# Seven block products in place of eight for part of an MLP's second projection, inside a fused two-layer kernel on one core

## The reference, cut to what matters

```python
def squared_relu_mlp(h, w1, w2):            # h 256x2048, w1 2048x8192, w2 8192x2048
    return jnp.square(jax.nn.relu(h @ w1)) @ w2

x = x + squared_relu_mlp(h, w_mlp_in[l], w_mlp_out[l])
return rmsnorm(x, norm_final)               # then the second layer starts
```

## Time and profile before

| | |
|---|---|
| median of 3 runs (lowest, highest) | 1685.77 us (1685.72, 1685.93) |
| the profiled execution's own time | 1685.47 us |
| its span, first to last instruction | 1683.7 us |
| TensorE matmul busy, share of span | 1674.5 us, 99% |
| weight load (PEld), DVE, ACT, POOL busy | 86%, 67%, 49%, 3% |
| granted TensorE clock | 1.00 of full |
| DMA: moved, mean rate | 361.47 MB, 215 GB/s |

### The profile page before, as it was taken

The page is one execution under the profiler, slowest core; times in us unless marked ns, Lnnn a source line. Parts: engine busy times, 40 slices in busy tenths (PEclk is TensorE's granted clock), DMA queues, the critical chain, the costliest instruction groups (busy, mean ns, idle before and its releaser), DMA issues.

```text
span 1683.7 us, 25495 instructions
## 1 busy us (share of the span) xinstructions
PE 1674.5 (99%) x9397; PEld 1454.5 (86%) x9397; DVE 1125.7 (67%) x1148; ACT 823.6 (49%) x1085; POOL 56.8 (3%) x64
## 2 busy tenths in 40 slices
PE   9999999999999999999999999999999999999998
PEld 7888888888888888888888888799999988888886
DVE  5554546557877777777877777775675556757754
ACT  5645754554445444444445445454444454444443
POOL 1000000000000000000000000000000001101100
PEclk9999999999999999999999999999999999999999
DMA  9643545567777787767777777675555655555562
GB/s 305 221 132 115 189 138 175 163 206 268 260 258 261 271 277 279 252 231 279 266 266 257 265 260 254 215 233 170 171 167 176 196 188 190 179 194 173 196 205 88
DMA packets 171691, 361.47 MB, mean 215 GB/s; under 512 B 11008, under 2 KB 17472, under 8 KB 171344
## 3 DMA queue, kind: packets, MB, share of 16 engines
q1 hardware_dynamic: 169392, 352.37, 62.7%
q0 software_dynamic: 2064, 7.56, 1.3%
q10 hardware_dynamic: 144, 0.26, 0.0%
HBM read 358.00 MB, written 2.15 MB: 214 GB/s over the span
## 4 chain that ended last, share of the span: by engine, by line
PE 98%; DVE 1%; issue 1%; ACT 0%; POOLq 0%; POOL 0%; ACTq 0%; DVEq 0%
PE G L759 31%; PE S L759 13%; PE S L773 12%; PE G L773 12%; PE G L742 10%; PE G L776 6%; PE S L776 6%; PE S L712 2%; PE G L748 1%; PE S L1144 0%; PE S L797 0%; DVE window_sums L1849 0%; PE S L1137 0%; PE S L1123 0%; PE S L1011 0%
## 5 line engine op out<-in xcount | busy, mean ns | idle before, releaser
L1462 DVE TENSOR_TENSOR w_lo<-raw,w_hi 128x1024 fp32r<-128x1024 f32 (+1 forms) x573 | 702.7, 1244 | 403.1 <-ACT w_hi L1178 402.5
L1178 ACT ACTIVATE w_hi<-raw 128x1024 fp32r<-128x1024 f32 (+1 forms) x574 | 588.5, 1045 | 519.5 <-PE G L759 131.0
L759 PE MATMUL G<-w_hi,X_pair 128*128 128x512 f32 (+2 forms) x1456 | 444.6, 384 | 0.0
L759 PEld LDWEIGHTS G<-w_hi,X_pair 128*128 128x128 f32 x1456 | 269.6, 188 | 55.2 <-issue 3.3
L759 PE MATMUL G<-w_lo,X_pair 128*128 128x512 f32 (+2 forms) x728 | 276.8, 380 | 0.0
L773 PE MATMUL S<-Y_pair,w_hi 128*128 128x512 f32 x768 | 267.0, 390 | 0.0
L773 PE MATMUL G<-Y_pair,w_hi 128*128 128x512 f32 x768 | 266.8, 390 | 0.0
L776 PE MATMUL G<-Y_pair,w_lo 128*128 128x256 f32 x768 | 216.6, 282 | 0.0
L776 PE MATMUL S<-Y_pair,w_lo 128*128 128x256 f32 x768 | 216.6, 282 | 0.0
L742 PE MATMUL G<-Y_pair,w_hi 128*128 128x256 f32 x1088 | 194.0, 280 | 1.3 <-DVE Y_pair L1578 1.2
L773 PEld LDWEIGHTS S<-Y_pair,w_hi 128*128 128x128 f32 x768 | 144.2, 188 | 30.3
(11 more groups left out here) (349 smaller groups left out, 1464.4 us busy)
## 6 DMA issues: line engine op xcount, KB each, us to landing
raw<-in_w_in SPq DMA_DIRECT2D x142, 512.0 KB, 4.4
raw<-in_w_mlp_in SPq DMA_DIRECT2D x128, 512.0 KB, 5.5
raw<-in_w_mlp_out SPq DMA_DIRECT2D x128, 512.0 KB, 6.7
ada_w<-in_w_ada SPq DMA_DIRECT2D x64, 768.0 KB, 4.9
raw<-in_w_out SPq DMA_DIRECT2D x64, 512.0 KB, 4.4
raw<-in_w_merge SPq DMA_DIRECT2D x64, 512.0 KB, 4.3
raw<-in_w_branch_attn SPq DMA_DIRECT2D x16, 512.0 KB, 4.3
raw<-in_w_branch_pool SPq DMA_DIRECT2D x16, 512.0 KB, 6.2
```

The lines of the kernel that those rows point to most:

```text
L759: ins = nc.tensor.matmul(token_bank(bank, tt)[:, 0:n], a[:, c0 + c, tok], w[:, s % SPLIT, c, 0:n], start=first and c == 0 and k == 0, stop ...
L1178: nc.scalar.activation(w_hi[:, s % SPLIT, :, 0:n], raw[:, k, :, 0:n], ACT.Copy).then_inc(hi_ready, 1)
L1462: nc.vector.tensor_tensor(w_lo[:, s % SPLIT, :, 0:n], raw[:, k, :, 0:n], w_hi[:, s % SPLIT, :, 0:n], ALU.subtract).then_inc(lo_ready, 1)
```

## The change

The second projection into output columns 0 and 1 (16 of the 32 subs of a quarter's second half) is regrouped into two **sets** of 11 subs; the first projection and output columns 2 and 3 keep their form. A set covers 4 of the 8 row blocks of 256. Two of these row blocks, with both column blocks and both token halves, form a 2x2 by 2x2 block product, done by Strassen's (Winograd's form) seven products instead of eight; a product takes one token half (or a sum of hidden blocks) against one weight block or a sum of weight blocks, so 2 chunks x 3 = 6 matmuls. The other two row blocks are done as before (subs N1A, N1B, N0A, N0B of 12 matmuls). A quarter has 70 subs instead of 64, and every sub, short or long, needs its hi and lo part.

- Sums of hidden blocks: DVE (`sum_x`, 4 operations), ACT (`sum_hi`), DVE (`sum_lo`, 2 operations), once a set.
- Sums of weight blocks: ACT writes a negated copy of a block (`neg`, 4 a set), POOL issues a DMA that adds another block of the weights from the device memory onto it (`add_to`, `accum_op`). They form a chain: -B11+B12 = T1, -T1+B22 = T2, -T2+B21 = T4, and apart from it -B22+B12 = T3. Block B12 is not loaded by SP.
- The seven products stay in separate banks over both sets; DVE combines them in the quarter's second half (`mixA` to `mixG`, A on ACT).
- The square of the positive part moves from DVE (in `up`) to two operations on ACT (in `hid`).
- The sums of squares for the final norm are taken in the last quarter only (`norm_sums`, at slots 58, 60, 61, 66 and 69).
- The operations and loads of the modulation are put at other slots; the fold moves to slot 64, `SPLIT_AT` to 66.
- 70 is no multiple of 4, so from sub 60 on (`SKIP_AT`) the `w_hi`/`w_lo` buffers are numbered two further on: subs 60 and 61 reuse the buffers of subs 58 and 59.
- Apart from the MLP: at the kernel's start the transposition `turn_x(1)` moves ahead of the first lo matmuls of sub 0.
- ACT's P2 is written out for the last quarter (`peeled`), SP's and POOL's for all four.

```diff
-SPLIT_AT = 60
+SPLIT_AT = 66
...
-ADA_OPS = [0, 2, 4, 6, 7, 9, 11, 13, 14, 16, 18, 20, 21, 23, 25, 27, 28, 30, 32, 34, 35, 37, 39, 41, 42, 44, 46, 48,
-           49, 51, 53, 55]
-ADA_LOADS = [5 + 7 * _v // 2 for _v in range(16)]
-MLP_SUBS, MERGE_SUBS = 8 * len(ALL), 3 * len(ALL)
+ADA_OPS = [0, 1, 2, 3, 4, 5, 6, 8, 10, 12, 13, 14, 16, 17, 18, 19, 20, 21, 22, 24, 26, 28, 29, 30,
+           56, 57, 58, 59, 60, 61, 62, 63]
+ADA_LOADS = [1, 3, 11, 13, 15, 18, 22, 24, 27, 29, 31, 34, 55, 56, 61, 63]
...
+SKIP_AT = UP + MIXED + 6
...
+SLOT_SPLIT = [V1, N1A, N1B, V3, N0A, V7, V2, N0B]
+NEGATED = [(26, 0, 1), (28, 0, 3), (30, 0, 2), (34, 1, 1), (35, 0, 4), (38, 1, 3), (39, 1, 2), (43, 1, 4)]
+ADDED_AT = {1: (0, 1), 2: (1, 1), 3: (0, 1), 4: (1, 0)}
...
+NORM_SUMS = {("P2", 58): "sums0", ("P2", 60): "sums1", ("P2", 61): "sums2", ("P2", SPLIT_AT): "sums3_0",
+             ("P2", MLP_SUBS - 1): "sums3_1"}
...
-for _j in range(4):
-    stage("P2", 8 * _j + 7, f"up{_j}", A=1, D=2)
-    stage("P2", 8 * _j + 8, f"hid{_j}", A=1, D=1)
-stage("P2", 34, "mlp_rms", D=3)
...
-        stage("P2", 58, "ada_fold", D=2)
-    if _n < 3:
-        stage("P2", 39 + 8 * _n, f"down{_n}", A=4, D=4)
-stage("P2", SPLIT_AT, "down3_0", P=1, A=2, D=2)
-stage("P2", SPLIT_AT, "fs0", D=2, G=1)
-stage("P2", MLP_SUBS - 2, "down3_1", D=2)
-stage("P2", MLP_SUBS - 1, "down3_sq", A=2)
...
+for _s in range(MLP_SUBS):
+    for _g in range(SETS):
+        if _s == 16 * _g + 9:
+            stage("P2", _s, f"sum_x{_g}", D=4)
+        if _s == 16 * _g + 10:
+            stage("P2", _s, f"sum_hi{_g}", A=1)
+        if _s == 16 * _g + 11:
+            stage("P2", _s, f"sum_lo{_g}", D=1)
+    for _j in range(4):
+        if _s == 8 * _j + 7:
+            stage("P2", _s, f"up{_j}", A=1, D=1)
+        if _s == 8 * _j + 8:
+            stage("P2", _s, f"hid{_j}", A=3, D=1)
+    for _at, _g, _k in NEGATED:
+        if _s == _at and _at < UP + SET_SUBS:
+            stage("P2", _s, f"neg{_k}_{_g}", A=1)
+_set = UP + SET_SUBS
+stage("P2", _set + V1, "mixA", A=1)
+stage("P2", _set + V1, "neg4_1", A=1)
+stage("P2", _set + N1B, "mixB", D=2)
+stage("P2", _set + V6, "mixC", D=2)
+stage("P2", _set + V7, "mixD", D=2)
+stage("P2", _set + V4, "mixE", D=2)
+stage("P2", UP + MIXED, "mixF", D=2)
+stage("P2", UP + MIXED + 1, "mixG", D=2)
+stage("P2", UP + MIXED + 7, "down2", D=2)
+stage("P2", 64, "ada_fold", D=2)
+stage("P2", SPLIT_AT, "down3_0", P=1, D=1)
+stage("P2", MLP_SUBS - 2, "down3_1", D=1)
...
+        def split_of(s, loop):
+            return (s + 2 * (in_mlp(loop) and s - PHASE["P2"][0] >= SKIP_AT)) % SPLIT
...
+            def mixed(s, loop, i, j):
...
+                ws = split_of(s, loop)
+                def product(bank, a_hi, a_lo, c):
+                    for m, (a, w) in enumerate(((a_hi, w_hi), (a_hi, w_lo), (a_lo, w_hi))):
+                        ins = nc.tensor.matmul(PROD[bank], a, w[:, ws, c, :],
+                                               start=g == 0 and k == OPENS[bank] and c == 0 and m == 0,
+                                               stop=g == 1 and k == CLOSES[bank] and c == SUB - 1 and m == 2)
+                    return ins
...
+                    if k in NORMAL:
+                        p, banks = NORMAL[k]
+                        ch = 8 * g + SUB * p + c
+                        for tt in range(NT):
+                            tok = slice(P * tt, P * (tt + 1))
+                            ins = product(banks[tt], x_hi[:, ch, tok], x_lo[:, ch, tok], c)
+                    elif k in (V1, V2, V4):
+                        ch = 8 * g + (0 if k == V1 else SUB) + c
+                        tok = slice(P, TOK) if k == V4 else slice(0, P)
+                        ins = product(PRODUCT[k], x_hi[:, ch, tok], x_lo[:, ch, tok], c)
+                    else:
+                        m = {V5: 0, V6: 1, V7: 2, V3: 3}[k]
+                        ins = product(PRODUCT[k], x_sum_hi(g, m)[:, c, :], x_sum_lo(g, m)[:, c, :], c)
+                ins.then_inc(used, 1)
             def gemm_pair(s, loop, slot, lhs, c0, banks, first, last):
...
                     nc.scalar.activation(w_hi[:, s, 0, 0:n], raw[:, s, 0, 0:n], ACT.Copy).then_inc(first_hi, 1)
                     act.wait_ge(raw_in[s], 16)
                     nc.scalar.activation(w_hi[:, s, 1, 0:n], raw[:, s, 1, 0:n], ACT.Copy).then_inc(hi_ready, 1)
                     return
-                act.wait_ge(raw_in[k], v if loop is None else loop[0] * (16 * loop[1] // RAW) + v)
+                r = raw_of(s, loop)
+                g, k = set_sub(s, loop)
+                if k in SET_SUMS:
...
+                else:
+                    act.wait_ge(raw_in[r % RAW], raw_count(r, loop))
                 if s >= SPLIT:
-                    act.wait_ge(used, count(s, loop, 1 - SPLIT))
-                nc.scalar.activation(w_hi[:, s % SPLIT, :, 0:n], raw[:, k, :, 0:n], ACT.Copy).then_inc(hi_ready, 1)
+                    here = s - PHASE["P2"][0] - SKIP_AT if in_mlp(loop) else -1
+                    act.wait_ge(used, count(s, loop, 1 - (2 if here in (0, 1) else 6 if here in (2, 3) else SPLIT)))
...
+                elif name[:3] == "neg":
+                    k, g = int(name[3]), int(name[5])
+                    at2, loop = PHASE["P2"][0], (i, MLP_SUBS)
+                    set_at = at2 + UP + SET_SUBS * g
+                    if k in (1, 3):
+                        slot = 0 if k == 1 else 3
+                        act.wait_ge(raw_in[slot], raw_count(at2 + UP + 8 * g + slot, loop))
+                        from_ = raw[:, slot, :, :]
+                        if k == 3:
+                            act.wait_ge(lo_ready, count(set_at - SET_SUBS + V7 if g else at2 + UP + SET_FROM[V7] - RAW, loop, 1))
+                        elif g:
+                            act.wait_ge(ada_free, i * 32 + 3 + 2 * ADA_EARLY)
+                    elif k == 2:
+                        act.wait_ge(t1_in, i * 32 + 16 * (g + 1))
+                        from_ = w_added(g, 1)
+                        if g == 0:
+                            act.wait_ge(dve_side, done("D", "sum_lo1", i))
+                    else:
+                        act.wait_ge(t2_in, i * 32 + 16 * (g + 1))
+                        from_ = w_added(g, 2)
+                        if g == 0:
+                            act.wait_ge(lo_ready, count(set_at + V5, loop, 1))
+                    nc.scalar.activation(w_added(g, k), from_, ACT.Copy, scale=-1.0).then_inc(act_side, 1)
+                elif name == "mixA":
+                    act.wait_ge(used, count(PHASE["P2"][0], (i, MLP_SUBS), UP + SET_SUBS + V1 + 1))
...
                     act.wait_ge(dve_side, done("D", f"up{b}", i))
+                    nc.scalar.activation(right[:, :, :], right[:, :, :], ACT.Relu).then_inc(act_side, 1)
+                    act.wait_ge(act_side, step("A", name, 1, i))
+                    nc.scalar.activation(chunked(hid), right[:, :, :], ACT.Square).then_inc(act_side, 1)
+                    act.wait_ge(act_side, step("A", name, 2, i))
                     nc.scalar.activation(x_hi[:, 4 * b:4 * b + 4, :], chunked(hid), ACT.Copy).then_inc(act_side, 1)
-                elif name in ("down3_0", "down3_sq"):
-
-                    tt, from_ = (0, "down3_0") if name == "down3_0" else (1, "down3_1")
...
+            def norm_sums(name):
+                last = QUARTERS - 1
+                n = int(name[4])
+                for k, tt in ([(k, tt) for k in range(2) for tt in range(NT)] if n < 3 else [(0, int(name[-1])), (1, int(name[-1]))]):
+                    if n == 1 and not k:
+                        act.wait_ge(squares_made, 4)
+                    if k:
+                        act.wait_ge(scaled_made, 2 * n + tt + 1)
+                    else:
+                        act.wait_ge(dve_side, done("D", "mixG", last) if n < 2 else step("D", "down2", tt + 1, last) if n < 3
+                                    else step("D", f"down3_{tt}", 1, last))
+                    src = x_nf[:, tt, :] if k else x[:, tt, NW * n:NW * (n + 1)]
+                    c = 64 + 10 * k + 5 * tt + n
+                    nc.scalar.activation(src if k else hid[:, tt, :], src, ACT.Square, scale=D_MODEL ** -0.5,
+                                         accum_out=stat[:, c:c + 1]).then_inc(squares_made, 1)
             act.wait_ge(zeros_ready, 1)
             nc.scalar.activation(small[:, 95:96], soft[:, 0:1], ACT.Copy)
...
+                elif name[:5] == "sum_x":
+                    h = chunked(hid)
+                    a11, a12, a21, a22 = (h[:, 0:2, 0:P], h[:, 2:4, 0:P], h[:, 0:2, P:TOK], h[:, 2:4, P:TOK])
+                    s1, s2, s3, s4 = (x_sum[:, k, :, :] for k in range(4))
+                    dve.wait_ge(act_side, step("A", f"hid{2 * int(name[5])}", 2, i))
+                    nc.vector.tensor_tensor(s1, a21, a22, ALU.add).then_inc(dve_side, 1)
+                    nc.vector.tensor_tensor(s3, a21, a11, ALU.subtract).then_inc(dve_side, 1)
+                    dve.wait_ge(dve_side, step("D", name, 1, i))
```

(62 more changed lines are left out.)

243 lines of the change are left out of this document (167 added, 76 removed).

## The result

The changed kernel takes 1725.51 us (median of 4, 1725.23 to 1726.74), the one before 1685.74 beside it: 1.024 times as long (95% interval 1.0227 to 1.0253). Forecast were 1702 us and, for eight in ten, a range of 1682 to 1724. The direction and nearly all places were right, the size was not: +39.8 us instead of +16.6.

What follows compares the result with a forecast made beforehand. TensorE was taken as the bound, if lo parts stay ready. Three quarters at +1.6 (+4.7), the last +12.2 and the start -0.3 gave +16.6, so 1702 us; eight in ten: 1682 to 1724.

Steps and rivals of the forecast that it cites:

- start: Kernel start: the moved transposition fills a gap of 0.4 us before the first lo matmuls, -0.3 us (0 to -0.4).
- step 1: First set's start: queued work on ACT and DVE makes sub 36's lo part late, +0.2 us a quarter (0 to 1).
- step 2: Weight sums: ACT waits for adding transfers, delaying subs 42, 43 and 47 by 1.3, 0.5 and 0.4; 2.2 us a quarter.
- step 3: Fold at slot 64: queued on DVE ahead of lo68, making it 1.9 us late in each quarter (1 to 3).
- step 4: Last quarter's norm sums: squares delay subs 62, 64, 65 by 2.6, 2.1, 4.4; with sub 68's 3.3, 12.5 us.
- What bounds the kernel: Whole run: TensorE is busy 1674.5 of 1683.7 us; fewer matmuls shorten it only if lo parts stay ready.
- L: Weight sums: an adding transfer's time from issue to landing, taken as 7.5 us (bounds 4.4 and 11), 6.2 free.
- the clock: TensorE's granted clock: should it fall from 1.00 after a 4 us gap, the last quarter adds 1 to 2 us.
- slow accumulations: Rival, 18%: adding transfers land in 9.5 us or more; 1718 us at 9.5, over 1725 beyond 10.
- What costs nothing: Hidden-block sums, the mixes, 24 more conversions and unrolled code fit into spare time, without added waits.
- Quick accumulations: Rival, 14%: adding transfers land in under 6.2 us, so the weight sums cost no wait; 1693 us.
- the matmuls set the end: Rival, 12%: buffer lead at slots 57 to 68 suffices, the whole 10.9 + 0.3 saving shows; 1674.3 us.

Runs made afterwards that it cites:

- e11: The kernel before with only the change's start edit, turn_x(1) ahead of the first lo matmuls: 1684.84 us beside 1685.04, ratio 0.9999.
- e3: The changed kernel with the modulation's fold moved from slot 64 to slot 67, behind the quarter's last lo part: 1719.19 us, ratio 1.0199.
- e4: The changed kernel with the final norm's multiplications and squares of output columns 0 to 2 cut to 8 columns, output wrong: 1722.91 us, ratio 1.0222.
- e5: The changed kernel with 18 useless matmuls ahead of sub 42 of each quarter's first set, output wrong: 1720.48 us, ratio 1.0202.
- e2: The changed kernel with POOL's 32 weight DMAs as plain copies, nothing added, output wrong: 1701.31 us, ratio 1.0098.
- e6: The changed kernel with the second set's negations later, so T4 of the first set no longer directly follows another adding transfer: 1724.28 us, ratio 1.0225.
- e1: The changed kernel with one first-set sub converting T2 instead of T4, so nothing waits for T4's landing, output wrong: 1724.03 us, ratio 1.0226.
- e7: The changed kernel with the first set's chain earlier, T4 in its own buffer, second set's later, fold at 67, norm sums at 56, 62, 65: 1709.84 us.
- e9: e7 with POOL's weight DMAs as plain copies, sums and output wrong: 1693.43 us, ratio 1.0049 to the kernel before.
- e12: The changed kernel with weight sums subtracted on DVE, without negated copies or adding DMAs, fold and norm sums as in e7: 1699.35 us, ratio 1.0087.

## Why the prediction was wrong

By the forecast's terms, in us over the whole run:

| term | forecast | measured | from |
|---|---|---|---|
| 48 matmuls fewer | -10.9 | -10.9 | x9349 against x9397 |
| start | -0.3 | open, 0 to -0.5 | e11 |
| step 1, sub 36 | +0.8 | +1.2 | 0.2 in three quarters, 0.5 in the last |
| step 2, weight sums | +8.8 | +19.3 | stops at sub 42 |
| step 3, fold | +9.0 | +8.5 | stops at sub 68; e3 |
| step 4, norm sums, without the fold's sub 68 | +9.1 | +5.9 | two stops; e4 |
| slow matmuls behind stops | 0 | +13.2 | e5 |

- **What bounds the kernel: right.** TensorE without waits and two engines near the edge of their lead. Every stop but the 0.9 at the next phase's start lies where a step had put one. The readings hold with two remarks: the two starts of the earlier trace rows lie ahead of the MLP, whose own second projection has the same pace, 0.2267 us (650 to 690 us); and two waits of TensorE reach 1.5 us, not one.
- **Two terms failed: L in step 2, and the clock.** Together they are 23.7 us more than forecast; all else came out within 4. L was taken as 7.5, between SP's 6.7 and the 8.0 of one POOL transfer, and was 11.05. The queues had been laid out right: 6.2 us are free, so sub 42 is 4.85 late; measured 4.9, 5.0, 4.9, 4.5. The order that the step had laid out has T1 of the second set issued 1.9 us ahead of this one, with plain loads at the same moment, and no row of before had such a case. e2 shows that the adding is most of it: without it the same pair lands in 4.0 and 6.9, and the DMA engines' share is 0.75 instead of 1.09. How the rest divides between the transfer ahead and the plain loads is open (e6). The step's follow-ons, 0.5 at sub 43 and 0.4 or more at sub 47, didn't show behind the stop of sub 42; they do where that stop is gone, 0.5 at sub 43 in e2 and 4.2 to 5.2 at sub 47 in e1. The rival "slow accumulations", with its "over 1725 beyond 10", is what happened, and had deserved more than its 18%; e1 and e6 show that it isn't the accident of one slot. That its number fits the measured 1725.5 is in part luck: it held follow-ons that didn't show and no clock, and the clock's 13.2 us came in their place.
- **The clock was the larger miss.** It was 0 in the sum, and a remark gave it 1 to 2 us, in the last quarter alone. It came to 13.2, the largest single difference: taken off the measured time it leaves 1712 us, an estimate, and inside the range. Eight of the twelve stops, all of 2.3 us and more among them, drew slow matmuls; those of 1.9 (third quarter), 1.6, 0.9 and 0.5 drew none. Less stopping drew less (slow matmuls in e2 6.4, e7 7.1, e9 4.1, the constant 1.7 included), and as much in shorter pieces too (e6: stops 35.5, slow 12.2). That the clock falls after a stop of 4 us, the trace of before couldn't show; but a step that forecasts waits of several us should carry this as a term of its own.
- **Step 3: right in mechanism and size**, 1.9 forecast, 1.9, 3.1 and 1.9 measured; the 3.1 falls in the quarter where DVE stood 1.1 us for the modulation's load, the case named for the upper end. e3 shows the fold as its cause, and that some of it is needed again at the next layer's start.
- **Step 4: right in place, too high in size.** 2.6 was 2.3, 4.4 was 3.6, and 2.1 at sub 64 did not show in the change. Eight slow matmuls, 1.6 us, lie between the stops at subs 62 and 65 there and gave the queues the time back; in e2, e5 and e6, where none are slow in that place, a stop of 1.5 us stands at sub 64. I had added waits as though none of them relieved the next. The fold's 3.3 in this quarter was 1.6, and came to 3.1 in e4 and e6. e4 falsifies my later reading that the squares' own length was the whole price: it was less than half.
- **Step 1: right** in the change, with 0.2 in three quarters. Its place became the largest remaining one once the others were out of the way (e9, e12).
- **"What costs nothing" held:** no stop at the mixes or the hidden blocks' sums.
- **The rivals.** "Quick accumulations" and "the matmuls set the end" are excluded; even e9, with no adding at all, is 8 us over the kernel before. Nothing that I ran beats that kernel. About 2 us of what the stretch grew by are in no class. That the start's edit is worth 0.3 stays open.

## What to carry to other kernels

Price a transfer with all that is in flight when it is issued, not by the row of another one in calmer company, and ask first whether it reads what it writes: here an adding transfer took 1.6 times as long as a plain one, the first of a pair (6.2 against 4.0 us) and the second (11.05 against 6.9). Fewer matmuls are a gain only if the streams that feed them have room for the new small steps: 10.9 us saved here stood against 13 us of stops even in the best order without any adding. Where TensorE never waits, a new wait costs its length and then often, as here, the clock; check each new wait also against the one ahead of it, which may already have paid for it.

## What the hardware showed that I had not expected

- An adding DMA of 512 KB, issued by GpSimd, landed in 6.0 us at best (median of all 32: 8.5, longest 11.2; in e1 one took 13.6), the same plain copy in 3.9 (e2; median 6.5). The instruction that issues it takes 1.20 us instead of 0.72:

```profile
481.76 0.72 POOL L2260 DMA_DIRECT2D w_sum<-in_w_mlp_out  x1 [1.18 <-ACT w_sum L1571]
```

- The Trainium skill's formula for a transfer issued by GpSimd ("DMA: Bandwidth & Descriptors", "Anatomy of one DMA — SWDGE (gpsimd) path") gives 3.2 us for this size, an estimate; no transfer of the sums came to that, 3.9 for a plain one was the nearest. Its neighbour section ("Issuing engines are not separate DMA queues") has the transfers of all issuers run on the same DMA engines and interleave. The trace agrees: SP's loads issued at 482.50 and 486.26 in the changed kernel took 9.5 and 9.7 us, where 6.7 was the median before and 6.1 that of all 120 after.
- A subtraction of 128x1024 on GpSimd took 2.4 to 3.4 us, and the DVE operation beside it up to 3.44 instead of 1.22.
- Behind a stop of 4.7 us the granted clock fell from 1.00 to a mean of 0.76 in the 7 us that follow, with matmuls of 128x512 every 0.43 us instead of 0.227.
